# A two-layer hybrid decoder on one core: the 16 meta tokens' high and low parts as one stationary operand

## The chip, the core and the metric

The kernel runs on one core of a Trainium2 chip. The core has five engines that run side by side and meet only at semaphores: TensorE (PE, with its weight loads shown apart as PEld), VectorE (DVE), ScalarE (ACT), GpSimd (POOL) and SyncE (SP), which issues the loads of the weights. The metric is the device time of one execution in microseconds (us), and the time of a kernel is the median of several executions.

## What is computed

Two layers, each of them attention beside a convolution, then an MLP. The residual stream has 528 tokens: 16 learned meta tokens and the 512 of the sequence. The part that the change touches is the projection to queries, keys and values and what reads them:

```
u = rms_norm(h, norm_mix[l])
proj = u @ w_in[l]
glu_in, q, k, v, gates = jnp.split(proj, SPLITS, axis=-1)
...
q = apply_rope(rms_norm(q.reshape(B, Lp, N_HEADS, 2, HEAD_DIM), q_norm[l]), cos, sin)
k = apply_rope(rms_norm(k.reshape(B, Lp, N_HEADS, 2, HEAD_DIM), k_norm[l]), cos, sin)
...
o = diff_attention(q, k, v, lam)
...
h = h + merged @ w_o[l]
u = rms_norm(h, norm_mlp[l])
h = h + jnp.square(jax.nn.relu(u @ w_up[l])) @ w_down[l]
```

The width is 1024, there are 8 heads with two softmaxes each, and the output has the 512 sequence tokens of the last layer only.

## The kernel before

**Three products for one.** TensorE reads float32 operands here as float32r. To keep accuracy, every operand is held as a high part and a low part, and a product is made of three matmuls: high by high, low by high, high by low. `u[:, 0]` and `u[:, 1]` are the high and low parts of the normed input (transposed, channels on partitions), `w_hi` and `w_lo` those of a slab of weights, which is 1024 x 256 values. A slab comes by DMA into `w_raw`; for the query, key and value slabs ACT writes `w_hi` (`w_high_part`, a cast of 128 x 2048 values), and then POOL writes `w_lo` in 16 pieces (`split_low`) and announces the slab with `w_ready`. There are two buffers of each, so slab s+2 is split after slab s has been used, while slab s+1 is read.

**The tiles.** A pair of heads has three slabs, v, q and k. `b_tiles` lists tiles of tokens for each slab: tile 0 holds the 16 meta tokens, tiles 1 to 4 hold 128 tokens each. `b_tile` makes one: 8 blocks of the contraction by three matmuls, 24 in all, with a piece of `u` as the stationary operand (128 x 16 for tile 0, 128 x 128 for the others) and 256 columns of weights moving. The last layer has no meta queries, so meta tiles are 12 in layer 0 (v, q, k of four pairs) and 8 in layer 1 (v, k): 20 in all. Tiles go to two PSUM banks in turn. ACT evicts each (`b_evict`): a value tile with one scaled copy, a query or key tile with a copy to `raw` and four Squares with an accumulated sum, and then it releases the bank with `b_free`. After the last tile of a slab ACT casts the high part of slab s+2.

**The order.** Stage 0 of a layer is tiles alone, back to back. In stages 1 to 3 the tiles of pair p are strewn among the attention of pair p-1, and in stage 4 tiles of the gates (G) take their place. The order is written out in `MATRIX_ORDER`, and ACT follows the same list through `schedule`; DVE has a list of its own, `VECTOR_ORDER`, which the change leaves alone. In the list T is the next tile (T< and T> its halves), q and k0, k1 are transposes of rotated queries and keys, s, e, t, pv and y are the steps of a head: s01 is the scores of the pair's first head, group 1 (PE), e01 their exps (ACT), t00 and t01 the two halves of the transposes of the probabilities (PE, evicted by ACT to `a_t`), pv the product with the values, y the sums for the norm. Between s and e stands DVE's maximum (`maxima`, which ends with `nb`), and all scores use one pair of banks, so that scores of group n+1 wait until the exps of group n are done (`exp_done`). DVE's `combine` makes the probabilities after the third group. The keys take DVE and POOL after the last tile of the slab: norm statistics, `turn` on POOL, `rope` on DVE, and only then does POOL split the next slab.

The lines of the profile are those of the file before: L714 is the matmul of `b_tile`, L744 and L752 those of `scores`, L764 the transposes of the probabilities, L776 and L781 the product with the values, L702 sums over channels, L936 the eviction of a value tile, L945 and L949 of a query or key tile, L960 the cast of the high part, L995 the eviction to `a_t`, L973 and L978 the exps, L522 and L515 the low parts on POOL, L1235 the end of the keys' rotation on DVE.

## Time and profile before

| | |
|---|---|
| median of 3 runs | 1857.86 us (1855.82 to 1861.81) |
| the profiled execution | 1856.81 us, span 1855.0 us |
| granted TensorE clock | 0.999 of full speed |
| PE busy | 1831.2 us, 99% of the span, 12787 matmuls |
| PEld / POOL / DVE / ACT busy | 89% / 72% / 60% / 31% |
| query, key, value tiles (L714), PE busy | 337.1 + 259.7 us |

The profile is one execution. Busy time of matmuls overlaps, since a matmul is drained while the next one streams, so what a matmul costs is read from the distance between starts. In the chain of work that ended last PE holds 87% of the span and POOL 7%.

### The profile page before, as it was taken

How to read it: one execution, taken by the hardware profiler on the slowest of the kernel's cores; microseconds unless marked ns; L12 is line 12 of the kernel's file. 1: busy time of each engine (PE TensorE's matmuls, PEld its weight loads, DVE VectorE, ACT ScalarE, POOL GpSimd, SP SyncE). 2: the span in 40 equal slices, each digit the busy share in tenths (PEclk: the TensorE clock that was granted, in tenths of full speed). 3: DMA queues.
4: the chain of work that ended last, by engine and by line, in shares of the span. 5: the costliest groups of instructions: out<-in, count | busy, mean ns of one | idle time of the engine just before them, and what ended most of it. 6: DMA issues, size and time to landing. Idle time of an engine off the chain costs nothing.

```text
span 1855.0 us, 34632 instructions
## 1 busy us (share of the span) xinstructions
PE 1831.2 (99%) x12787; PEld 1652.2 (89%) x12787; DVE 1119.0 (60%) x1666; ACT 577.0 (31%) x1616; POOL 1333.3 (72%) x2400
## 2 busy tenths in 40 slices
PE   9999999999999999999999999999999999999999
PEld 9999888898999999999999998887768877888887
DVE  7998887877544333333468989888885433333233
ACT  4135565536332110101011246664362322010100
POOL 3767454646778888888898663436477799898985
PEclk9999999999999999999999999999999999999999
DMA  4221021112322222222232211111124222222222
GB/s 178 91 92 66 28 69 47 47 69 85 135 96 79 86 93 90 91 91 106 109 120 91 91 69 47 69 47 48 67 91 146 105 91 91 91 91 91 90 107 74
DMA packets 25550, 160.66 MB, mean 87 GB/s; under 512 B 3024, under 2 KB 3408, under 8 KB 7776
## 3 DMA queue, kind: packets, MB, share of 16 engines
q1 hardware_dynamic: 21888, 147.01, 22.4%
q10 hardware_dynamic: 3552, 12.15, 1.7%
q8 instruction: 73, 1.20, 0.3%
q14 instruction: 37, 0.30, 0.1%
HBM read 154.85 MB, written 4.29 MB: 86 GB/s over the span
## 4 chain that ended last, share of the span: by engine, by line
PE 87%; POOL 7%; DVE 2%; issue 2%; ACT 2%; POOLq 0%; DVEq 0%; ACTq 0%
PE psum L625 63%; PE psum L714 15%; POOL w_lo L515 4%; PE psum L744 2%; PE psum L776 2%; PE psum L764 1%; POOL w_lo L522 1%; POOL w_hi L513 1%; ACT e L978 1%; PE psum L752 1%; DVE mx L1259 1%; PE psum L646 1%; PE psum L821 1%; PE psum L793 1%; PE psum L632 0%
## 5 line engine op out<-in xcount | busy, mean ns | idle before, releaser
L625 PE MATMUL psum<-u,w_hi 128*128 128x264 f32 (+1 forms) x4416 | 900.5, 316 | 9.7 <-POOL w_lo L515 5.6
L515 POOL TENSOR_TENSOR w_lo<-w_raw,w_hi 128x128 fp32r<-128x128 f32 x1504 | 759.9, 543 | 7.8
L625 PEld LDWEIGHTS psum<-u,w_hi 128*128 128x128 f32 x4416 | 666.8, 189 | 68.1 <-issue 9.1
L625 PE MATMUL psum<-u,w_lo 128*128 128x264 f32 (+1 forms) x2208 | 558.8, 313 | 0.0
L522 POOL TENSOR_TENSOR w_lo<-w_raw,w_hi 128x128 fp32r<-128x128 f32 x640 | 314.3, 530 | 123.1 <-ACT w_hi L960 83.8
L625 PEld LDWEIGHTS psum<-u,w_lo 128*128 128x128 f32 x2208 | 362.5, 189 | 25.0
L714 PE MATMUL psum<-w_hi,u 128*128 128x256 f32 (+1 forms) x1856 | 337.1, 284 | 2.6 <-ACT v_sb L936 1.5
L467 DVE SCALAR_TENSOR_TENSOR psum<-xg,pvec,psum 128x512 f32<-128x512 f32 x440 | 300.9, 751 | 4.6 <-DVE xg L1399 2.2
L714 PEld LDWEIGHTS psum<-w_hi,u 128*128 128x128 f32 (+1 forms) x1856 | 264.8, 172 | 11.5 <-issue 3.1
L714 PE MATMUL psum<-w_lo,u 128*128 128x256 f32 (+1 forms) x928 | 259.7, 280 | 0.0
L1562 DVE TENSOR_TENSOR relu<-relu 128x528 f32<-128x528 f32 (+1 forms) x64 | 66.2, 1034 | 234.8 <-ACT u L1154 119.7
L1152 ACT ACTIVATE relu<-psum 128x528 f32<-128x528 f32 (+1 forms) x64 | 38.7, 605 | 459.9 <-PE psum L625 459.9
L513 POOL TENSOR_SCALAR w_hi<-w_raw 128x2048 fp32r<-128x2048 f32 x94 | 180.4, 1919 | 0.0
L512 POOL TENSOR_TENSOR tick<-ones 128x1 f32<-128x1 f32 x94 | 19.8, 211 | 218.8 <-PE psum L625 196.4
L625 PE MATMUL psum<-hid_b,w_hi 128*128 128x264 f32 (+1 forms) x768 | 163.9, 322 | 0.1
L714 PEld LDWEIGHTS psum<-w_lo,u 128*128 128x128 f32 (+1 forms) x928 | 159.7, 172 | 3.7
L1591 DVE TENSOR_TENSOR down_tmp<-psum,r_inv 128x512 f32<-128x512 f32 (+1 forms) x56 | 39.1, 699 | 190.3 <-PE psum L625 190.3
L567 POOL TENSOR_TENSOR rtmp<-raw,tabs 128x640 f32<-128x640 f32 x16 | 25.0, 1562 | 153.1 <-DVE q_scale L1221 101.9
L625 PEld LDWEIGHTS psum<-hid_b,w_hi 128*128 128x128 f32 x768 | 118.7, 188 | 12.0 <-issue 0.6
L625 PE MATMUL psum<-hid_b,w_lo 128*128 128x264 f32 (+1 forms) x384 | 102.4, 321 | 0.0
L978 ACT ACTIVATE e<-psum,nb,q_scale 128x272 f32<-128x272 f32 (+4 forms) x144 | 83.8, 585 | 35.8 <-DVE nb L1265 35.8
L960 ACT CAST w_hi<-w_raw 128x2048 fp32r<-128x2048 f32 x40 | 76.6, 1915 | 48.6 <-PE psum L625 48.6
(190 smaller groups left out, 1963.0 us busy)
## 6 DMA issues: line engine op xcount, KB each, us to landing
w_raw<-w_slabs SPq DMA_DIRECT2D x135, 1024.0 KB, 4.9
h<-x_t SPq DMA_DIRECT2D x4, 528.0 KB, 7.2
h<-x_t ACTq DMA_DIRECT2D x1, 2112.0 KB, 10.7
h_spill<-h ACTq DMA_DIRECT2D x8, 264.0 KB, 2.2
h<-h_spill ACTq DMA_DIRECT2D x1, 2112.0 KB, 10.4
out<-h SPq DMA_DIRECT2D x8, 256.0 KB, 2.0
r_b<-r_rows ACTq DMA_DIRECT2D x1, 1584.0 KB, 6.5
r_b<-r_rows ACTq DMA_DIRECT2D x1, 1536.0 KB, 7.4
```

Source lines behind the costliest of these rows:

```text
L467: return nc.vector.scalar_tensor_tensor(out=done if ends else acc, in0=x, scalar=w, in1=done if begins else acc, op0=ALU.mult, op1=ALU.add)
L513: chain.link(nc.gpsimd.tensor_scalar(w_hi[:, b, :], w_raw[:, b, :], 1.0, 1.0, ALU.mult, ALU.mult))
L515: last = nc.gpsimd.tensor_tensor(w_lo[:, b, c:c + P], w_raw[:, b, c:c + P], w_hi[:, b, c:c + P], ALU.subtract)
L522: last = nc.gpsimd.tensor_tensor(w_lo[:, b, c:c + P], w_raw[:, b, c:c + P], w_hi[:, b, c:c + P], ALU.subtract)
L625: last = nc.tensor.matmul(psum[:, 2 * slot + j, 0:n], w[:, b, cut], src[:, part, kc, at0:at0 + n], start=(kc == 0 and m == 0), stop=(kc == ...
L714: last = nc.tensor.matmul(psum[0:tn, n % 2, 0:2 * P], u[:, part, kc, t0:t0 + tn], w[:, b, kc * 2 * P:(kc + 1) * 2 * P], start=(kc == 0 and ...
L744: nc.tensor.matmul(psum[0:tn, banks[c], at0:at0 + k1 - k0], qk[rows64, 0, hh % 2, qp, t0:t0 + tn], qk[rows64, 1, hh % 2, kp, k0:k1], start ...
L960: nc.scalar.copy(w_hi[:, b, :], w_raw[:, b, :]).then_inc(w_high, 1)
L978: ins = nc.scalar.activation(e[0:tn, c, E_OFF[i]:E_OFF[i] + w], psum[0:tn, banks[c], S_AT[i]:S_AT[i] + w], ACT.Exp, bias=nb[0:tn, c, i:i + ...
L1152: nc.scalar.activation(row(relu[:, j, :], layer), a_ps(layer, j), ACT.Relu).then_inc(a_free[j], 1)
L1562: link(V.tensor_tensor(relu2[:, lo:lo + n], relu[:, j, lo:lo + n], relu[:, j, lo:lo + n], ALU.mult))
L1591: announce(dve, V.tensor_tensor(row(down_tmp[:], layer), a_ps(layer, j), row(r_inv2[:], layer), ALU.mult), a_free[j], a_read(layer, A_MLP ...
```

## The change

The meta tokens are taken out of `b_tiles`, which now has tiles 1 to 4 of each slab. For v, q and k of layer 0 and v and k of layer 1 a meta product is opened ahead of tile 1 (`b_open`): the stationary operand is `meta_u`, 128 x 32, the high parts of the 16 tokens beside their low parts, and it meets `w_hi` and `w_lo`, 16 matmuls in place of 24. That gives 32 rows, 16 from the high parts and 16 from the low ones. ACT copies them to `meta_low` (`meta_evict`). A float32 matmul with two 16 x 16 identities stacked as the stationary operand (L744 of the new file) then adds the two halves into columns 256 to 511 of the bank of tile 2, right behind tile 2's first matmul, and tile 2's eviction takes the 16 rows along. `meta_low` and the stacked identities are float32, so that matmul is a plain float32 one.

Three things come with it. Each product with meta tokens holds one of the two banks from its opening until ACT has copied it; tile 1 goes to the other bank and tile 2 to that one. The cast for slab s+2 moves: where the following slab has meta tokens, ACT makes it behind `meta_evict` of that slab and not behind the last tile of its own. And `MATRIX_ORDER` is written anew for the stages "first" and "mid".

```diff
 def b_tiles(layer):
-    return [("v", t) for t in range(NTOK)] + [("q", t) for t in q_tiles(layer)] + [("k", t) for t in range(NTOK)]
+    return [(what, t) for what in "vqk" for t in range(1, NTOK)]
...
-MATRIX_ORDER = [{"first": "T q T T T k0 T< s00 k1 e00 T> T s01 T< e01 T> T s02 T< e02 T> T T< t00 s10 t01 e10 T> T s11 e11 pv0 T< s12 e12 T> y0 T T< t10 T> t11",
-     "mid": "T T pv- T q T k0 T s00 e00 T T s01 T< e01 y- T> k1 s02 e02 T T s10 t00 T< t01 e10 T> T s11 T< e11 T> T< s12 e12 pv0 T> T< y0 t10 T> t11",
+MATRIX_ORDER = [{"first": "T< q T> T T k0 T< s00 k1 e00 T> T< s01 T> e01 T s02 T< e02 T> T T< t00 s10 t01 e10 T> s11 e11 pv0 T< s12 e12 T> y0 T T< t10 T> t11",
+     "mid": "T pv- T q T k0 T s00 e00 T s01 T< e01 y- T> k1 s02 e02 T T s10 t00 T< t01 e10 T> s11 T< e11 T> T< s12 e12 pv0 T> T< y0 t10 T> t11",
...
-     "mid": "T T< pv- T> q T k0 T s00 k1 T< e00 T> y- s01 T< e01 T> T< s02 e02 T> T s10 t00 T< t01 e10 T> pv0 s11 T< e11 T> T s12 y0 e12 T T T< t10 T> t11",
+     "mid": "T pv- T< q T> k0 T s00 k1 T< e00 T> y- s01 T< e01 T> T< s02 e02 T> T s10 t00 t01 T< e10 T> pv0 s11 T< e11 T> s12 y0 e12 T T T< t10 T> t11",
...
+            def b_parts(n, b, t, first, last, opened):
+                t0, tn = TOK[t]
+                for k in range(first, last):
+                    part, w = [(0, w_hi), (1, w_hi), (0, w_lo)][k % 3]
+                    kc = k // 3
+                    done = nc.tensor.matmul(psum[0:tn, B_BANK[n], 0:2 * P], u[:, part, kc, t0:t0 + tn], w[:, b, kc * 2 * P:(kc + 1) * 2 * P],
+                                            start=k == 0, stop=k == 3 * NT - 1)
+                    if k == 0 and opened:
+                        nc.tensor.matmul(psum[0:META, B_BANK[n], 2 * P:4 * P], meta_low[0:2 * META, 2 * P:2 * P + META], meta_low[0:2 * META, 0:2 * P], start=False, stop=False)
+                return done
+            def b_open(layer, n, b):
...
+                for kc in range(NT):
+                    for w in (w_hi, w_lo):
+                        last = nc.tensor.matmul(psum[0:2 * META, bank, 0:2 * P], meta_u[:, kc, :], w[:, b, kc * 2 * P:(kc + 1) * 2 * P],
+                                                start=kc == 0 and w is w_hi, stop=kc == NT - 1 and w is w_lo)
+                last.then_inc(meta_full, 1)
...
+            def meta_evict(layer, pair, j, what):
...
+                act.wait_ge(meta_full, m + 1)
+                nc.scalar.copy(meta_low[0:2 * META, 0:2 * P], psum[0:2 * META, B_BANK[n + 1], 0:2 * P]).then_inc(meta_out, 1)
+                while high_due:
+                    w_high_part(layer, high_due.pop())
...
                 if t == NTOK - 1:
-                    w_high_part(layer, s + 2)
+                    following = "qkv"["vqk".index(what)]
+                    if with_meta(layer, following) and (what != "k" or pair < 3):
+                        high_due.append(s + 2)
+                    else:
+                        w_high_part(layer, s + 2)
...
+                act.wait_ge(u_ready, (layer * 2 + 1) * NT)
+                nc.scalar.copy(meta_u[:].rearrange("p k (a m) -> p k a m", a=2), u[:, :, :, 0:META].rearrange("p a k m -> p k a m")).then_inc(meta_in, 1)
...
+                announce(dve, V.tensor_tensor(meta_low[0:2 * META, 2 * P:2 * P + META], ident[0:2 * META, 0:META], ident[0:2 * META, META:2 * META], ALU.add), meta_sum, layer + 1)
```

On ACT, the place of the keys of pair 1 in layer 0 (stage 2), from the end of the fourth query tile to the first exp of the pair's second head. `a_t` is the transposed probabilities, `squares` a scratch of the norm sums. Before:

```order
L949 ACTIVATE squares,ssq<-psum 128x64 x3
L960 CAST w_hi<-w_raw 128x2048 [waits w_landed1]
L995 COPY a_t<-psum 128x512 [waits t_full] x2
L995 COPY a_t<-psum 128x256 [waits t_full]
L997 COPY a_t<-psum 16x16
L995 COPY a_t<-psum 16x512 [waits t_full]
L978 ACTIVATE e,es<-psum,nb,q_scale 128x272 [waits t_full,max_ready]
```

And now:

```order
L1031 ACTIVATE squares,ssq<-psum 128x64 x3
L1081 COPY a_t<-psum 128x512 [waits t_full] x2
L989 COPY meta_low<-psum 32x256 [waits meta_full]
L1046 CAST w_hi<-w_raw 128x2048 [waits w_landed1]
L1081 COPY a_t<-psum 128x256 [waits t_full]
L1083 COPY a_t<-psum 16x16
L1081 COPY a_t<-psum 16x512 [waits t_full]
L1064 ACTIVATE e,es<-psum,nb,q_scale 128x272 [waits t_full,max_ready]
```

The cast has moved from ahead of the first `a_t` copies to between the two halves of them, behind a copy that waits for the opened keys.

On ACT again, the keys of pair 1 in layer 1 (stage 2), from the product with the values (evicted to `o_t`) to the exps of the second head's group 1, which begin with those of `s_tail`. Before:

```order
L949 ACTIVATE squares,ssq<-psum 128x64 x3
L960 CAST w_hi<-w_raw 128x2048 [waits w_landed1]
L1014 ACTIVATE o_t<-psum,sub_g 128x512 [waits t_full]
L1015 ACTIVATE o_sq<-psum 128x512
L973 ACTIVATE e,es<-s_tail,nb,q_scale 128x16 [waits max_ready]
```

And now:

```order
L1031 ACTIVATE squares,ssq<-psum 128x64 x3
L1100 ACTIVATE o_t<-psum,sub_g 128x512 [waits t_full]
L1101 ACTIVATE o_sq<-psum 128x512
L989 COPY meta_low<-psum 32x256 [waits meta_full]
L1046 CAST w_hi<-w_raw 128x2048 [waits w_landed1]
L1059 ACTIVATE e,es<-s_tail,nb,q_scale 128x16 [waits max_ready]
```

The cast stands directly ahead of these exps now, and it waits for PE to have opened the keys, which PE does after the scores of group 1.

On PE, the start of tile 2 of the values in stage 0 of layer 0, with the new matmul behind the first of the tile:

```order
L741 MATMUL psum<-w_hi,u 128x256 [waits meta_out,meta_sum,w_ready]
L744 MATMUL psum<-meta_low 16x256
L741 MATMUL psum<-w_hi,u 128x256
L741 MATMUL psum<-w_lo,u 128x256
L741 MATMUL psum<-w_hi,u 128x256 x2
```

In the tile before the change the first two rows of `w_hi` followed each other without it.

## Rows read from the trace of the kernel before

**Rows 1.** The page, part 1: busy time, share of the span and instructions.

```profile
PE 1831.2 (99%) x12787; PEld 1652.2 (89%) x12787; DVE 1119.0 (60%) x1666; ACT 577.0 (31%) x1616; POOL 1333.3 (72%) x2400
```

**Rows 2.** Groups by shape: line, stationary and moving sizes, count | busy us, mean ns | idle before.

```profile
L714 PE MATMUL psum<-w_hi,u 128*16 128x256 f32 x320 | 58.1, 282 | 0.8 <-POOL w_lo L522 0.8
```

**Rows 3.** Timeline of PE, stage 0 of layer 0: start, us, line, shapes, count.

```profile
122.87 0.40 PE L714 MATMUL psum<-w_hi,u 128*16 128x256 f32 x2
...
125.66 0.40 PE L714 MATMUL psum<-w_hi,u 128*128 128x256 f32 x2
...
128.49 0.40 PE L714 MATMUL psum<-w_hi,u 128*128 128x256 f32 x2
```

**Rows 4.** Timelines of PE and PEld where plain float32 matmuls stand.

```profile
432.80 7.37 PE L702 MATMUL psum<-ln_sq,ones 128*128 128x264 f32 x32
439.81 0.85 PE L625 MATMUL psum<-u,w_hi 128*128 128x264 f32 x4
...
1186.67 3.37 PE L776 MATMUL psum<-a_t,v_sb 128*128 128x512 f32 x10
1189.97 0.97 PE L744 MATMUL psum<-qk 64*128 64x512 f32 x6
...
197.70 0.19 PEld L776 LDWEIGHTS psum<-a_t,v_sb 128*128 128x128 f32 x1 [0.24 <-issue]
```

**Rows 5.** Waits of PE over the whole span: in total, times, longest.

```profile
PE psum L744 <- ACT e L978: 3.1, 9, 0.5
...
PE psum L714 <- ACT v_sb L936: 1.5, 2, 0.7
...
PE psum L714 <- POOL w_lo L522: 1.1, 2, 0.8
```

**Rows 6.** Timelines of POOL and PE, stage 1 of layer 0: the second query slab.

```profile
162.83 7.60 POOL L522 TENSOR_TENSOR w_lo<-w_raw,w_hi 128x128 fp32r<-128x128 f32 x16 [4.75 <-DVE raw L1235]
...
170.49 0.41 PE L714 MATMUL psum<-w_hi,u 128*16 128x256 f32 x2 [0.82 <-POOL w_lo L522]
```

**Rows 7.** Timelines of ACT and PE, stage 1 of layer 0: last exp of group 0, scores.

```profile
195.45 0.18 ACT L978 ACTIVATION_READ_ACCUMULATOR e<-psum,nb,q_scale 16x1 f32 x1
...
196.19 0.97 PE L744 MATMUL psum<-qk 64*128 64x512 f32 x6
```

**Rows 8.** Timeline of ACT, stage 2 of layer 0, around the first keys.

```profile
255.07 1.93 ACT L960 CAST w_hi<-w_raw 128x2048 fp32r<-128x2048 f32 x1
256.87 1.11 ACT L995 COPY a_t<-psum 128x512 f32<-128x512 f32 x2
258.60 0.37 ACT L995 COPY a_t<-psum 128x256 f32<-128x256 f32 x1 [0.63 <-PE psum L764]
...
259.54 0.57 ACT L978 ACTIVATE e<-psum,nb,q_scale 128x272 f32<-128x272 f32 x1
...
262.15 0.19 ACT L978 ACTIVATION_READ_ACCUMULATOR e<-psum,nb,q_scale 16x1 f32 x1
```

**Rows 9.** Timeline of PE in the same stretch.

```profile
256.52 0.48 PE L714 MATMUL psum<-w_hi,u 128*16 128x256 f32 x2
...
258.00 1.02 PE L764 MATMUL psum<-ident,e 128*128 128x128 f32 x7
258.78 0.48 PE L714 MATMUL psum<-w_hi,u 128*16 128x256 f32 x2
...
263.18 0.97 PE L744 MATMUL psum<-qk 64*128 64x512 f32 x6
```

**Rows 10.** Timelines of PE and ACT, stage 2 of layer 1, around the first keys.

```profile
1190.96 0.42 PE L714 MATMUL psum<-w_hi,u 128*16 128x256 f32 x2
...
1196.71 0.81 PE L744 MATMUL psum<-qk 64*128 64x400 f32 x6
...
1193.17 0.40 ACT L973 ACTIVATE e<-s_tail,nb,q_scale 128x16 f32<-128x16 f32 x1 [1.24 <-DVE nb L1265]
...
1195.37 0.19 ACT L978 ACTIVATION_READ_ACCUMULATOR e<-psum,nb,q_scale 128x1 f32 x1
```

**Rows 11.** Timeline of PE, stage 1 of layer 1: second transposes right behind the first.

```profile
1125.38 1.00 PE L764 MATMUL psum<-ident,e 128*128 128x128 f32 x6 [0.38 <-ACT a_t L995]
```

More of the change, by code:

```diff
@@ L422, in b_read_wait @@
             for k in range(2):
-                eng.wait_ge(b_free[k], (n + 1 - k) // 2)
+                eng.wait_ge(b_free[k], B_USES[n][k])
         def round_wait(eng, n):
@@ L704, in channel_sums @@
                 last.then_inc(done, 1)
-            def b_tile(layer, n, b, t, half):
+            def b_parts(n, b, t, first, last, opened):
                 t0, tn = TOK[t]
-                if n >= 2 and half != 1:
-                    pe.wait_ge(b_free[n % 2], n // 2)
-                for kc in range(NT) if half is None else range(half * NT // 2, (half + 1) * NT // 2):
-                    for m, (part, w) in enumerate([(0, w_hi), (1, w_hi), (0, w_lo)]):
-                        last = nc.tensor.matmul(psum[0:tn, n % 2, 0:2 * P], u[:, part, kc, t0:t0 + tn], w[:, b, kc * 2 * P:(kc + 1) * 2 * P],
-                                                start=(kc == 0 and m == 0), stop=(kc == NT - 1 and m == 2))
+                for k in range(first, last):
[6 more added lines that the diff above has]
+                return done
@@ new lines, in b_tile @@
+            def b_tile(layer, n, b, t, half, meta):
+                bank = B_BANK[n]
+                opened = int(meta is not None and t == 2)
+                if meta is not None and t == 1:
+                    if half != 1:
+                        b_open(layer, n + 1, b)
+                    cuts = 0, 0, 3 * NT
+                else:
+                    cuts = 0, 3 * NT // 2, 3 * NT
+                lo, hi = cuts[1 if half == 1 else 0], cuts[1 if half == 0 else 2]
+                if lo == hi:
+                    return
+                if opened and half != 1:
+                    pe.wait_ge(meta_sum, layer + 1)
+                    pe.wait_ge(meta_out, meta + 1)
+                elif lo == 0 and B_USES[n][bank]:
+                    pe.wait_ge(b_free[bank], B_USES[n][bank])
+                last = b_parts(n, b, t, lo, hi, opened)
@@ L866, in _ @@
                             pe.wait_ge(w_ready, slab + 1)
-                            b_tile(layer, n + x, slab % 2, t, c[0])
+                            b_tile(layer, n + x, slab % 2, t, c[0], metas_before(layer, stage, what) if with_meta(layer, what) else None)
                         elif step == "gate":
@@ L929, in b_evict @@
                     act.wait_ge(b_full, n + 1 - (layer * N_QKV + 3 * pair + "vqk".index(what)))
+                meta = with_meta(layer, what) and t == 2
+                bank = B_BANK[n]
                 if what == "v":
-                    if t == 0 and (layer or pair > 1):
+                    if t == 1 and (layer or pair > 1):
                         before = ("pv", layer, 2 * pair - 3) if pair > 1 else ("pv", layer - 1, HEADS - 1)
```

58 lines of the change are left out of this document (48 added, 10 removed), and 2 rows, old and new, of the table MATRIX_ORDER.

## The prediction

> **What bounds the kernel now.** I read part 1 of the page first: PE is busy for 99% of the span [rows 1], so a microsecond of PE work is worth up to a microsecond, and any pause of PE costs its length. Next the waits of PE: those in the attention stages are few and short, at most 0.8 us each [rows 5]. They name what stands close behind PE there: the exps on ACT, the value evictions on ACT, the low parts on POOL. PE is thus the bound, but with little cover left on the others. The question for this change is which of the exp chains, that run scores, maximum, exps, next scores, lose the tiles that hide them. I answer it place by place from the timelines of PE and ACT. All sums are against the profiled execution of 1856.81 us, which lies 1.05 us below the median; the same difference is then put on the median.
>
> **What the matmuls give back.** A meta tile is 24 matmuls with a 16-column stationary operand, 320 + 160 of them in all for 20 tiles [rows 2]. It takes 125.66 - 122.87 = 2.79 us, a tile of 128 tokens 128.49 - 125.66 = 2.83 us [rows 3]. So a matmul of 256 columns costs 0.1165 to 0.118 us whatever the width of the stationary operand, and 32 columns will cost the same. Opening takes 16 of them: 8 fewer are 0.94 us per meta tile, 18.8 us for 20. The Trainium skill (TensorE: Matmul & The Clock Gate, Back-to-back issue gap) gives the columns over 2.4 GHz plus 2.5 ns, 0.109 us for 256; by that alone the 20 tiles would give 17.5 us, but the trace's distance of 0.1175 us decides.
>
> **What the identity matmul takes.** The trace has no lone float32 matmul of 256 columns between float32r ones. Plain float32 matmuls are recorded as two each. The 32 of L702 take 439.81 - 432.80 = 7.01 us, 0.219 us each for 264 columns, so 0.438 us for one matmul and 0.427 us for 256 columns. Five of L776, with 1792 columns, take 1189.97 - 1186.67 = 3.30 us, where 1792 columns at that rate are 2.97: 0.07 us more each [rows 4]. Coming back to float32r costs about 0.07 us: the half tile at 256.52 takes 1.48 us for 12 matmuls [rows 9], where 12 x 0.1175 are 1.41. I take 0.55 us. From below the bound is 0.43, the streaming alone. From above it is 0.99: 0.43 plus two pauses of 0.24 us, as weight loads of L776 show them [rows 4], plus 0.08. The Trainium skill (FP8 and Floating Point Precision, TensorE Precision Notes) has true float32 as four passes through the array, 0.427 us for 256 columns; with nothing for the change of type the sum would be about 1.8 us lower than mine.
>
> Net, a meta tile that is wholly on the path gives 0.94 - 0.55 = 0.39 us.
>
> **Stage 0.** Tiles back to back. No wait for a bank is recorded there, and the only one between tiles that is, behind value evictions, comes from stages 2 and 3 [rows 5]; I take it that tile 2's eviction, longer by the meta rows, still fits into the 2.8 us tile behind it. Three meta tiles in layer 0 and two in layer 1 give 5 x 0.39 = -1.95 us.
>
> **Stage 1, values and queries.** The value tile gives nothing. The second query slab is split only after the keys' rotation, which hangs on the end of the previous key tile: POOL starts at 162.83, behind L1235, and PE waits 0.82 us for it at 170.49 [rows 6]. A shorter value slab makes that wait longer by as much. In layer 1 the same wait is 0.3 us (the second of the two in [rows 5]) and takes the same gain. The query tile of layer 0 gives -0.39.
>
> **Stage 1, keys, layer 0.** Between the second head's scores of group 0 and group 1 there were 36 matmuls of tiles and there will be 24: -1.41 us of cover. The exps end at 195.45 + 0.18 = 195.63, PE started group 1 at 196.19 [rows 7], 0.56 us later. For the way of a semaphore I allow 0.14 us (POOL's end at 170.43 and PE's start at 170.49 show 0.06 [rows 6]). PE will come about 1.4 us earlier and wait 0.95 to 1.0 us. Keys: -0.94 + 0.55 + 0.97 = +0.58.
>
> **Stages 2 and 3, layer 0.** The values gain more than tiles. Before, both banks were full of value tiles that ACT may not evict until the product with the values is done, and PE waited 0.7 us for that, twice [rows 5]. The opened meta product is copied without waiting, so its bank is free: -0.39 - 0.73 = -1.12. Queries: -0.94, and the identity matmul falls where PE waited 0.34 us for exps anyway (the mean of nine such waits [rows 5]), so it costs 0.21: -0.73. Keys are the place that decides. Before, ACT made the cast at 255.07, ahead of the `a_t` copies, where it had time, copied the second half of `a_t` at 258.60 when PE delivered it, and began the exps at 259.54 [rows 8]. Now the cast stands behind the copy of the opened keys. PE opens at 256.52, and 16 matmuls with the switch take 1.95, so until 258.47; the last starts at 258.35, lasts 0.28 [rows 2] and ends at 258.63, the copy starts at 258.67, the cast 0.26 later at 258.93 (a copy of 0.37 us [rows 8], of which 0.1 overlaps the next instruction, as the cast's last 0.13 does), and the next instruction 1.80 us after it (256.87 - 255.07) at 260.73. The copies take 0.94 (259.54 - 258.60), the exps 2.80 (to 262.34) [rows 8]: they end at 264.47, and PE may go on at 264.61. PE itself arrives at 263.18 - 0.94 = 262.24 [rows 9]. A new wait of 2.37 us. In the group after, the identity matmul takes the place of a wait of 0.38. Keys: -0.94 + 2.37 + 0.17 = +1.60. A stage: -1.12 - 0.73 + 1.60 = -0.25, two stages -0.5.
>
> **Layer 1, keys of stage 1.** No 12 matmuls are lost ahead of group 1; the identity falls on a wait of 0.46 us (the longest in [rows 5]), and a wait of about 0.3 for the probabilities comes up since 12 matmuls fewer lie between group 2 and their transposes. I put -0.4.
>
> **Stages 2 and 3, layer 1.** Values: -0.39. The halves of the transposes now follow each other. Where they did so before, PE waited 0.38 us for ACT [rows 11], and the four transposes of the last round, which wait for a second copy, took some 0.4 more: +0.8. Keys: the scores of group 1 start at 1189.97 [rows 4], the opening at 1190.96 [rows 10] and lasts 1.90; copy at 1193.06, cast at 1193.32, and the exps of group 1 can start at 1195.12. Before, they started at 1193.17 and ended at 1195.56, 2.39 later [rows 10]. So they end at 1197.51, PE may go on at 1197.65, and it arrives at 1196.71 - 0.94 = 1195.77: a new wait of 1.88. Keys: -0.94 + 0.55 + 1.88 = +1.49. A stage: -0.39 + 0.8 + 1.49 = +1.9, two stages +3.8.
>
> **The rest.** 20 copies to `meta_low` (0.26 us each, as above) and 20 evictions of meta rows lie on ACT, 31% busy [rows 1]; beyond the places above they are covered. Without cover one costs 0.3 us. The copy to `meta_u` and the sum of identities stand on ACT and DVE between the GLU steps; together 0 to 0.4 us, I take 0.1. The casts come 0.4 to 6 us later, and POOL still ends these slabs 3 us or more before PE wants them. Query slabs hang on the rotation, not the cast. Stage 4 and the MLP follow PE and move with it.
>
> **Sum.** -1.95 (stage 0) - 0.39 + 0.58 (stage 1, layer 0) - 0.5 - 0.4 + 3.8 + 0.1 = +1.2 us. So 1858.0 us for the profiled execution and 1859.1 for the median. The matmuls give back 18.8 us, the identity matmuls take 11, and new waits take the rest.
>
> **Rivals.**
> *The cast does no harm.* If the exps behind it are not late (ACT is nearer to PE's end of the opening than I read, or there is cover that I miss), four waits go, 2 x 2.37 + 2 x 1.88 = 8.5 us: 1850.6. For it: the lists were written anew at just these places. Against it: the order of instructions on ACT is fixed, and the cast needs 1.8 us [rows 8] between two things that PE waits for.
> *The identity matmul is dear.* At 0.99 us each, 0.44 more on the 14 that are wholly exposed and the 4 that only fill a wait: 18 x 0.44 = 7.9 us, 1867.0, slower. For it: the weight loads of L776 do pause 0.24 us [rows 4], and a float32 matmul among float32r ones changes type twice. Against it: the five of L776 pay 0.07 us each. It decides from about 0.8 us each, where the sum passes 0.3%.
> *The saving isn't there.* If a matmul with 32 columns and alternating `w_hi` and `w_lo` cost more than 0.1175 us, say 0.13, 320 of them add 4 us: 1863. Rows 3 speak against it.
>
> **How the numbers follow.** About 0.3% (5.6 us) is what a measurement of this kernel can tell from no change. Forecast, with the sizes of its waits a little off, 0.55: 1855.5 to 1863. Harmless casts 0.17. Dear identities 0.12. Dearer opening 0.06. The remaining 0.10 is a wait I have not found, or a place where less is lost, spread over both sides. For a range with no more than 2 in 10 outside, I go down to the second case and leave out the third and most of the tail above: 1850.0 to 1865.0. Faster by over 0.3% (below 1852.3): 0.18. Slower by over 0.3% (above 1863.4): 0.18. Within: 0.64.
>
> **What would show it.** In the profile after, PE's busy time falls by some 8 us while the span stays. PE waits for the exps in total of some 6 to 9 us, against 3.1, with waits of 2.4 us in stages 2 and 3 of layer 0 at group 1 of the second head and of 1.9 us in layer 1 at its group 2. The waits for the value eviction are gone. The wait for the second query slab in layer 0 grows to about 1.2 us. The distance from tile 2's first matmul to its third is 0.55 us longer. I am wrong if the casts don't stand ahead of late exps, or if the identity matmul costs above 0.8 us.

## The result: slower by 0.7%

The kernel after the change takes 1871.19 us (median, 1870.47 to 1873.31), the kernel before 1856.93 us over all its runs beside it; the ratio is 1.0072 (95% interval 1.006 to 1.0084). The forecast was 1859.1 us with a range of 1850.0 to 1865.0, and the measured time lies 6.2 us above that range. A repeat (e9 below) gave 1869.92 against 1857.34, ratio 1.0069.

Part 1 of the page of the kernel after, against [rows 1]:

```profile
PE 1837.3 (98%) x12667; PEld 1651.6 (88%) x12667; DVE 1120.1 (60%) x1668; ACT 584.3 (31%) x1638; POOL 1333.0 (71%) x2400
```

PE has 120 instructions fewer and is busy 6 us longer. So waits alone don't explain the time: the same work has become dearer somewhere. The waits of PE after, against [rows 5] (L806 is the scores, L826 the transposes of the probabilities, L755 the opening):

```profile
PE psum L806 <- ACT e L1064: 9.4, 8, 2.1
...
PE psum L826 <- ACT a_t L1081: 1.9, 5, 0.4
...
PE psum L755 <- POOL w_lo L551: 0.8, 1, 0.8
```

The waits for exps have grown from 3.1 to 9.4 us in total, and the one for value evictions is gone, both as forecast in kind. The chain behind the long waits is the one of the prediction too. Timeline of ACT after, stage 2 of layer 0, against [rows 8]: start, us, line, operation.

```profile
255.94 0.36 ACT L989 COPY meta_low<-psum 32x256 f32<-32x256 f32 x1 [1.11 <-PE psum L755]
256.20 1.90 ACT L1046 CAST w_hi<-w_raw 128x2048 fp32r<-128x2048 f32 x1
258.01 0.36 ACT L1081 COPY a_t<-psum 128x256 f32<-128x256 f32 x1
...
258.81 0.57 ACT L1064 ACTIVATE e<-psum,nb,q_scale 128x272 f32<-128x272 f32 x1
...
261.43 0.19 ACT L1064 ACTIVATION_READ_ACCUMULATOR e<-psum,nb,q_scale 16x1 f32 x1
```

PE in the same place, against [rows 9]:

```profile
259.33 0.28 PE L741 MATMUL psum<-w_lo,u 128*128 128x256 f32 x1
261.76 1.62 PE L806 MATMUL psum<-qk 64*128 64x512 f32 x6 [2.14 <-ACT e L1064]
...
263.94 1.03 PE L744 MATMUL psum<-meta_low 32*16 32x256 f32 x2
264.90 0.58 PE L741 MATMUL psum<-w_hi,u 128*128 128x256 f32 x1
...
270.90 0.82 PE L806 MATMUL psum<-qk 64*128 64x400 f32 x6
```

The exps end at 261.62, and the scores begin 0.14 us later, after a wait of 2.14 us. What the prediction doesn't have is on the same rows. The six score matmuls take 1.62 us where they took 0.97 [rows 9], the identity matmul is recorded with 1.03 us (0.60 in stage 0), and the 35 tile matmuls from 264.90 to 270.90 take 6.00 us where 35 x 0.1175 are 4.11. PE ran at half clock behind the pause. Stretches of 12 us from each of the four long waits, after, with the first of them before as the last line: busy us of PE, PEld, DVE, ACT, POOL, then the granted clock.

```profile
261.00:273.00 12.00, 11.24 (x57) 8.53 (x58) 6.82 (x10) 6.27 (x39) 5.73 (x14) 0.72 0.26 89
332.00:344.00 12.00, 11.55 (x58) 9.04 (x59) 6.45 (x11) 5.98 (x38) 4.50 (x11) 0.72 0.25 87
1202.00:1214.00 12.00, 11.31 (x67) 10.01 (x68) 9.85 (x17) 5.25 (x33) 5.01 (x13) 0.72 0.25 87
1269.00:1281.00 12.00, 11.83 (x85) 11.04 (x86) 10.38 (x18) 5.94 (x41) 4.50 (x11) 0.86 0.25 87
```

```profile
261.00:273.00 12.00, 11.62 (x82) 9.43 (x81) 10.88 (x16) 8.40 (x45) 6.72 (x12) 1.00 0.26 87
```

A clock of 0.72 over 12 us is work for 3.4 us not done, 0.86 is 1.7 us. In slices of 4 us the clock reads 0.50 behind three of the waits, which is 1.2 GHz. That makes 3 x 3.4 + 1.7 = 11.9 us. The kernel before loses 1.7 us in this way, once, behind a wait of 2.37 us for DVE that ends at 31.37 us. But it also waits 1.83 us for POOL in the MLP of layer 1, as long as the two new waits of layer 1, and keeps the whole clock there. Both rows, and 12 us around each:

```profile
31.37 1.03 PE L625 MATMUL psum<-u,w_hi 128*128 128x264 f32 x3 [2.37 <-DVE glu_a L1390]
...
1390.24 0.73 PE L625 MATMUL psum<-u,w_hi 128*128 128x512 f32 x2 [1.83 <-POOL w_lo L515]
```

```profile
28.00:40.00 12.00, 9.63 (x68) 9.42 (x67) 6.48 (x9) 2.76 (x3) 5.98 (x11) 0.86 0.25 89
1387.00:1399.00 12.00, 10.17 (x45) 7.92 (x44) 6.38 (x9) 6.37 (x8) 9.88 (x20) 1.00 0.23 87
```

Lengths of the stretches between the same points of both kernels (us):

| stretch | before | after | difference | of it half clock | forecast |
|---|---|---|---|---|---|
| start to the first tiles | 108.75 | 107.42 | -1.33 | -1.7 | +0.1 |
| layer 0, stage 0 | 42.31 | 41.82 | -0.49 | 0 | -1.17 |
| layer 0, stage 1 | 62.17 | 62.87 | +0.70 | 0 | +0.19 |
| layer 0, stage 2 | 67.50 | 70.48 | +2.98 | +3.4 | -0.25 |
| layer 0, stage 3 | 68.23 | 71.85 | +3.62 | +3.4 | -0.25 |
| to the tiles of layer 1 | 699.99 | 700.06 | +0.07 | 0 | 0 |
| layer 1, stage 0 | 39.52 | 39.08 | -0.44 | 0 | -0.78 |
| layer 1, stage 1 | 58.80 | 58.23 | -0.57 | 0 | -0.4 |
| layer 1, stage 2 | 61.22 | 66.47 | +5.25 | +3.4 | +1.9 |
| layer 1, stage 3 | 62.58 | 65.89 | +3.31 | +1.7 | +1.9 |
| the rest | 583.93 | 584.13 | +0.20 | 0 | 0 |
| sum | 1855.0 | 1868.3 | +13.3 | +10.2 | +1.2 |

Without the clock the difference is 3.1 us, where the forecast had 1.2.

### The profile page after: what moved, and what is told of

Same layout as the page of the kernel before. It is cut to its first block, busy times and chain, and to the rows that moved or that the text cites. A ratio compares the mean times of both kernels' runs of the same rounds, so it can differ in the third digit from the quotient of the medians.

```text
span 1868.3 us, 34398 instructions
## 1 busy us (share of the span) xinstructions
PE 1837.3 (98%) x12667; PEld 1651.6 (88%) x12667; DVE 1120.1 (60%) x1668; ACT 584.3 (31%) x1638; POOL 1333.0 (71%) x2400
## 3 DMA queue, kind: packets, MB, share of 16 engines
q8 instruction: 72, 1.18, 0.3%
## 4 chain that ended last, share of the span: by engine, by line
PE 86%; POOL 6%; issue 2%; ACT 2%; DVE 2%; DMA 0%; POOLq 0%; DVEq 0%; ACTq 0%
PE psum L654 62%; PE psum L741 13%; POOL w_lo L544 4%; PE psum L838 2%; PE psum L806 2%; PE psum L755 2%; POOL w_lo L551 1%; PE psum L826 1%; ACT e L1064 1%; POOL w_hi L542 1%; PE psum L814 1%; PE psum L855 1%; PE psum L675 1%; PE psum L883 1%; PE psum L744 1%
## 5 line engine op out<-in xcount | busy, mean ns | idle before, releaser
L741 PE MATMUL psum<-w_hi,u 128*128 128x256 f32 x1536 | 294.1, 291 | 0.7 <-POOL w_lo L551 0.7
L741 PEld LDWEIGHTS psum<-w_hi,u 128*128 128x128 f32 x1536 | 242.9, 193 | 12.5 <-issue 11.2
L741 PE MATMUL psum<-w_lo,u 128*128 128x256 f32 x768 | 218.5, 284 | 0.0
L741 PEld LDWEIGHTS psum<-w_lo,u 128*128 128x128 f32 x768 | 148.5, 193 | 0.0
```

The costliest lines, as they stand in the source:

```text
L741: done = nc.tensor.matmul(psum[0:tn, B_BANK[n], 0:2 * P], u[:, part, kc, t0:t0 + tn], w[:, b, kc * 2 * P:(kc + 1) * 2 * P], start=k == 0, ...
```

## The experiments

My theory: the moved cast makes four pauses of PE (7.9 us), the pauses bring half clock behind them (10 to 12 us), and together with a dearer identity matmul this eats what the matmuls give back. Rivals: the clock falls because of something else in the changed kernel (the plain float32 matmul, the mix of types, the new order), or the pauses are only where the time happens to show.

**e1: the cast back.**

```diff
                 if t == NTOK - 1:
-                    following = "qkv"["vqk".index(what)]
-                    if with_meta(layer, following) and (what != "k" or pair < 3):
-                        high_due.append(s + 2)
-                    else:
-                        w_high_part(layer, s + 2)
+                    w_high_part(layer, s + 2)
```

> The kernel after the change, with ACT's cast of the high part put back to where it stood before: behind the last tile of its own slab, not behind the copy of the opened meta product. All else is as changed. My theory is that the 14 us come from the moved cast: four waits of PE for late exps (2.14, 2.14, 1.81 and 1.81 us in the profile after), and the half clock that the profile shows behind each of them (6.8 us of half clock three times and 3.4 us once, which costs up to 3.4 x 3 + 1.7 = 12 us). It expects those four waits to be under 0.5 us, the granted clock back at 0.998 or more, and 1851 to 1856 us. A rival, that the new order of the tiles and the plain float32 identity matmuls make the time and the cast only fell beside them, expects waits of the same sum somewhere else, or the half clock to stay, and 1864 us or more.

Measured: 1856.27 us (1854.08 to 1857.55), against 1857.12 for the kernel before beside it, ratio 0.9997 (0.9988 to 1.0007). The page's waits for exps, and 16 us around the first of the four places:

```profile
PE psum L806 <- ACT e L1060: 3.5, 8, 0.9
```

```profile
260.00:276.00 16.00, 15.40 (x107) 12.30 (x106) 13.51 (x24) 11.22 (x60) 6.60 (x12) 1.00 0.19 68
```

In layer 0 the waits shrink to 0.60 us, not quite under the 0.5 I had written; in layer 1 they are 0.15 us. The time lies 0.3 us above the 1851 to 1856 that I expected. The clock is whole at all four places. One edit on ACT takes back 14.9 us, all of the loss of 14.3. The moved cast is the cause; by which way it is not shown yet.

**e2 and e11: the pauses filled.** The casts stay where they do harm; PE only gets something to do while it waits. `fill` is 18 and 15 (layer 0, layer 1) in e2 and 9 and 7 in e11, in stages 2 and 3 for the keys.

```diff
+                for k in range(fill if meta is not None and t == 1 and half == 1 else 0):
+                    nc.tensor.matmul(psum[0:tn, bank, 0:2 * P], u[:, k % 2, k % NT, t0:t0 + tn], w_hi[:, b, k % NT * 2 * P:(k % NT + 1) * 2 * P], start=k == 0, stop=k == fill - 1)
                 last = b_parts(n, b, t, lo, hi, opened)
```

> The kernel after the change, with idle matmuls put in front of the four waits: ahead of the first key tile in stages 2 and 3, PE makes 18 (layer 0) or 15 (layer 1) redundant matmuls of the same shape and type as the tile's, 2.1 and 1.8 us of them, as long as the waits were; their result is overwritten. The casts stay where the change put them, the exps are as late as before. If the half clock is a consequence of PE standing still there, it goes: the waits fall to near 0, the granted clock is 0.998 or more, and although PE has 66 matmuls more to do the time is 9 to 12 us lower than the kernel after, 1859 to 1863 us. If the clock has another cause (the identity matmul, the mix of types), nothing is gained: 1870 to 1872 us with a clock of 0.994.

Measured: 1863.38 us (1859.66 to 1864.62), 7.8 us less than the kernel after, with 66 matmuls more. The same 16 us:

```profile
260.00:276.00 16.00, 15.99 (x112) 13.04 (x111) 11.94 (x23) 12.16 (x60) 7.49 (x16) 1.00 0.20 68
```

The clock is 1.00 at all four places. The gain is below the 9 to 12 us expected, since in the profiled execution PE lost 1.7 us each at two other places (near 32 us, as in the kernel before, and near 1396 us, behind a wait of 1.87 us for POOL that all kernels here have). The execution with the highest clock, 1.000, took 1859.66. Work in place of waiting keeps the clock, with the identity matmuls, the types and the order all left as changed. That excludes the first rival.

> The kernel after the change with half of the redundant matmuls ahead of the late scores: 9 in stages 2 and 3 of layer 0, 7 in those of layer 1, so that PE's four waits shrink to about 1.1, 1.1, 1.0 and 1.0 us while the scores start as late as ever. The whole fill left no wait there and no half clock and gave 1863.4 us. If it is enough to halve the pauses, the clock is whole again, 0.998 or 0.999, and the time is that of the whole fill, 1862 to 1864 us. If pauses of 1 us lose the clock as those of 2 us do (one of 1.07 us did so in the old kernel, and one of 1.70 us did not), it stays at 0.993 to 0.996 and 1867 to 1872 us.

Measured: 1864.55 us (1863.03 to 1867.45) at a clock of 0.996 to 0.998. Its waits are 1.07, 1.06, 0.97 and 0.99 us. Windows of 12 us from the first and from the last:

```profile
262.00:274.00 12.00, 11.79 (x76) 9.06 (x77) 9.41 (x19) 8.27 (x44) 4.28 (x11) 1.00 0.26 89
...
1260.00:1272.00 12.00, 11.49 (x69) 10.19 (x70) 10.03 (x18) 5.11 (x34) 4.83 (x12) 0.72 0.27 87
```

Three of the four pauses of 1 us cost nothing beyond themselves, and one cost 3.4 us. The median lies between the two expectations, 0.6 us above the range of the first: half the pause was usually short enough, not always.

**e4 and e7: pauses in the old kernel.** The kernel before, meta tiles and all, with small chained copies on ACT ahead of the second head's exps; `pad` is a scratch of its own. The counts shown are those of e4; e7 has 12, 12, 18 and 18.

```diff
             def exps(layer, hh, n):
...
+                for _ in range({(0, 3, 0): 10, (0, 5, 0): 6, (1, 3, 1): 14, (1, 5, 1): 10}.get((layer, hh, n), 0)):
+                    link(nc.scalar.copy(pad[:], ones[:, 0:32]))
                 act.wait_ge(max_ready, step + 1)
```

> The kernel before the change, whose meta tiles are untouched, with small chained copies on ACT ahead of the exps of the second head: group 0 of it in layer 0 (10 copies in stage 2, 6 in stage 3), group 1 in layer 1 (14 and 10). I estimate 0.3 us for each, so PE should wait for exps about 2.1 and 1.0 us in layer 0 and 2.0 and 0.8 us in layer 1, where before it waited less than 0.5. My theory, that a pause of PE is followed by half clock whatever the kernel does otherwise, expects half clock behind the long two at least, 1.7 to 3.4 us lost for each beyond the pause: 6 us of pauses and 4 to 10 us of clock, 1866 to 1872 us. The shorter two tell what a pause of 1 us does. The rival, that only the changed kernel's matmuls lose the clock, expects the pauses alone, 1861 to 1864 us, at a clock of 0.999.

Measured: 1862.22 us (1861.63 to 1863.71), clock 0.997 or 0.998. Two of its waits and the 12 us around each:

```profile
265.24 0.97 PE L745 MATMUL psum<-qk 64*128 64x512 f32 x6 [1.70 <-ACT e L981]
...
1200.54 0.81 PE L745 MATMUL psum<-qk 64*128 64x400 f32 x6 [1.07 <-ACT e L981]
```

```profile
264.00:276.00 12.00, 10.76 (x71) 8.54 (x72) 9.07 (x20) 8.94 (x47) 3.97 (x10) 1.00 0.26 88
...
1198.00:1210.00 12.00, 10.93 (x81) 10.50 (x80) 9.30 (x18) 7.37 (x40) 3.65 (x9) 0.86 0.26 87
```

My expectation failed: the time lies in the range that I had written for the rival (1861 to 1864), the longest pause kept the clock and a shorter one lost it. One loss of 1.7 us in the old kernel doesn't decide between the two. The copies were shorter than estimated, too (0.25 us each), so the pauses came out at 1.70, 0.70, 1.07 and none.

> The kernel before the change again with chained small copies on ACT ahead of the exps of the second head, now 12 in both stages of layer 0 and 18 in both of layer 1. The run with 10, 6, 14 and 10 copies gave waits of 1.70, 0.70, 1.07 and none, and half clock behind one of them alone, the 1.07 us in layer 1. Per copy that is 0.24 to 0.25 us, so these should give four waits of about 2.2, 2.2, 2.0 and 2.0 us, 8.4 us and a little more than the 7.9 us of the changed kernel. If such pauses lose the clock in the old kernel as in the new one, another 7 to 12 us come with them, the granted clock is 0.993 to 0.995 and the time 1872 to 1878 us. If the clock falls only sometimes, as the first run of this kind has it, 1867 to 1872. If the changed kernel's clock fell for another reason, 1865.5 us at 0.999.

Measured: 1869.88 us (1867.88 to 1871.07), ratio 1.0064 (1.0049 to 1.0079), clock 0.995 to 0.997. The waits are 2.21, 2.21, 2.08 and 2.08 us.

```profile
264.00:276.00 12.00, 11.53 (x65) 9.34 (x66) 8.07 (x16) 7.62 (x42) 2.68 (x7) 0.86 0.25 87
335.00:347.00 12.00, 11.60 (x79) 9.40 (x80) 9.63 (x21) 8.76 (x46) 2.57 (x7) 1.00 0.24 89
1203.00:1215.00 12.00, 11.29 (x70) 11.06 (x71) 9.37 (x17) 5.80 (x37) 0.81 (x2) 0.72 0.24 87
1270.00:1282.00 12.00, 11.80 (x89) 11.57 (x90) 10.36 (x19) 6.69 (x43) 0.29 (x1) 0.86 0.22 88
```

The old kernel, made to wait in the same places, is nearly as slow as the new one. Half clock came behind three of four pauses and cost 1.7 + 3.4 + 1.7 = 6.8 us. That is under the 7 to 12 that I expected for "as in the new kernel", and the time fits the middle case, 1867 to 1872: the clock falls often, not always. The rival's 1865.5 us at a clock of 0.999 is out.

**e3, e6 and e10: what the identity matmul costs.** Timeline of the kernel after, stage 0, tile 2 of the values:

```profile
112.07 0.28 PE L741 MATMUL psum<-w_hi,u 128*128 128x256 f32 x1
...
112.28 0.60 PE L744 MATMUL psum<-meta_low 32*16 32x256 f32 x2
112.81 0.19 PEld L741 LDWEIGHTS psum<-w_hi,u 128*128 128x128 f32 x1 [0.42 <-issue]
112.81 0.39 PE L741 MATMUL psum<-w_hi,u 128*128 128x256 f32 x1
...
113.05 0.28 PE L741 MATMUL psum<-w_lo,u 128*128 128x256 f32 x1
```

Three distances are long: 0.21 ahead of the matmul, 0.53 its own, 0.24 behind. Without the identity matmul the way from 112.07 to 113.05, 0.98 us, would be 2 x 0.1175. The price is 0.75 us, where the prediction had 0.55.

```diff
-        meta_low = at("meta_low", [P, 2 * P + META], F32, base)
+        meta_low = at("meta_low", [P, 2 * P + META], F32R, base)
```

> The kernel after the change, with meta_low and the stacked identities as float32r, so that the matmul that adds the halves goes through once and without a change of type. That rounds the meta tokens' queries, keys and values; nothing else is changed. It prices the identity matmul in place. The prediction put 0.55 us on it, the profile after shows about 0.76 in stage 0. As float32r it should cost about the 0.12 us of the others, 0.64 less by the profile's figure and 0.43 less by the prediction's. 20 of them, of which 14 to 18 stand on the path: 9 to 11.5 us less than the kernel after by the first, 6 to 8 by the second, and the stretch of stage 0 between tile 1's start and tile 3's shorter by 0.64 or 0.43 us. The waits behind the cast and the half clock stay, since the cast stays. If the identity were nearly free already, the time would stay at 1871.

Measured: 1864.86 us (1863.66 to 1865.55), 6.3 us less than the kernel after. The meta tokens' queries, keys and values are rounded here, and in e5, e8 and e12 below, which they are in neither of the two kernels; those times belong to a less exact computation.

```profile
112.43 0.28 PE L741 MATMUL psum<-w_hi,u 128*128 128x256 f32 x1
112.64 0.29 PE L744 MATMUL psum<-meta_low 32*16 32x256 f32 x1
112.86 0.39 PE L741 MATMUL psum<-w_hi,u 128*128 128x256 f32 x1
113.08 0.28 PE L741 MATMUL psum<-w_lo,u 128*128 128x256 f32 x1
```

From 112.43 to 113.08 are 0.65 us, so the price is 0.42, not the 0.12 of its neighbours. By its total the run would have confirmed a price of 0.55 with nothing left afterwards; the rows say 0.75 with 0.42 left. I went by the rows and asked what the 0.3 us are.

```diff
-                        nc.tensor.matmul(psum[0:META, B_BANK[n], 2 * P:4 * P], meta_low[0:2 * META, 2 * P:2 * P + META], meta_low[0:2 * META, 0:2 * P], start=False, stop=False)
+                        nc.tensor.matmul(psum[0:META, B_BANK[n], 2 * P:4 * P], meta_low[:, 2 * P:2 * P + META], meta_low[:, 0:2 * P], start=False, stop=False)
...
+                for p in (32, 64, 96):
+                    link(V.tensor_scalar(meta_low[p:p + 32, 0:2 * P], ident[p:p + 32, 0:1].to_broadcast([32, 2 * P]), 0.0, None, ALU.mult))
```

The sum of the identities is made over all 128 rows as well.

> The kernel after the change, with the identity matmul over 128 rows in place of 32: the stacked identities have zeros below row 32, and the rows of meta_low below 32 are zeroed by DVE once in a layer. It stays plain float32, and the result is the same. In the profile after, three distances around this matmul are longer than the others: 0.21 us ahead of it, 0.53 its own, 0.24 behind it, against 0.1175 each for the matmuls around; together it costs 0.75 us. As float32r the three are 0.21, 0.22 and 0.22, so 0.3 us of the price are left although type and passes are those of its neighbours. My reading is that these 0.3 us come from its 32 rows standing between matmuls of 128 rows, since the weight load of the next matmul starts only with that matmul. Then the distances next to it fall to about 0.12 and the price to 0.43 to 0.5 us: 20 x 0.25 to 0.3, of which 16 stand on the path, 4 to 5 us less than the kernel after, 1866 to 1867 us. If the price belongs to a lone matmul with another stationary operand, the distances stay and so does the time, 1870.5 to 1872 us.

Measured: 1866.35 us (1865.0 to 1870.33). The total is as expected, but the rows refute the reason:

```profile
114.09 0.28 PE L741 MATMUL psum<-w_hi,u 128*128 128x256 f32 x1
114.30 0.60 PE L744 MATMUL psum<-meta_low 128*16 128x256 f32 x2
114.84 0.38 PE L741 MATMUL psum<-w_hi,u 128*128 128x256 f32 x1
115.06 0.28 PE L741 MATMUL psum<-w_lo,u 128*128 128x256 f32 x1
```

The distances are 0.21, 0.54 and 0.22, as with 32 rows, and stage 0 takes 41.80 us against 41.82. The four executions had clocks of 0.993, 0.997, 0.996 and 0.995 and took 1870.33, 1865.0, 1865.56 and 1867.15 us. So I ran it again beside the kernel after.

> The kernel after the change as it is, on the chip and in the hours of the other three of this call. Its first runs had 1870.5 to 1873.3 us at a granted clock of 0.992 to 0.994; the runs with the same waits but another identity matmul had 0.993 to 0.997. If the half clock behind the waits comes every time, this gives 1870 to 1873 again. If it comes by chance from run to run, the clock is spread from 0.993 to 0.997 here too, and the time with it, 1865 to 1873 us, about 1.3 to 1.9 us for each thousandth of the clock.

> The kernel after the change with the plain float32 identity matmul over 128 rows, once more and beside the kernel after itself. The first time its median was 4.8 us below the kernel after, but its profile shows the three long distances around the identity unchanged (0.21, 0.54 and 0.22 us) and every stage as long as before the edit, and its four runs spread from 1865.0 to 1870.3 us as the clock went from 0.997 to 0.993. My reading now is that the row count does nothing while the matmul is plain float32, and that the 4.8 us are the clock's. Then it is within 2 us of the kernel after where both have the same clock. If the rows were worth something outside what the rows of stage 0 show, it is 4 to 5 us lower at the same clock.

Measured: 1869.92 us (1869.31 to 1870.52, clocks 0.993 to 0.995) for the kernel after and 1867.93 us (1866.34 to 1869.52, 0.994 to 0.996) for the one with 128 rows. The distance between the two has shrunk from 4.8 to 2.0 us, about what the clock differs by. In the kernel after the clock was not spread as far as 0.997: all its executions, eight now, lie between 0.992 and 0.995, which is the case "every time" of the expectation, with a median 0.1 us below the 1870 written there. The profiled spans less what half clock took (next table) are 1855.9 and 1857.1 us: no gain from the rows. Whether the last 2 us of the medians are chance stays open.

**e5, e8 and e12: together.**

> Two edits together on the kernel after the change: the cast back where it stood, and meta_low and the stacked identities as float32r, which rounds the meta tokens' queries, keys and values. Alone the first gave 14.9 us (1856.3) and the second 6.3 us (1864.9). If they are independent costs, as my theory has it, the sum is 1871.2 - 14.9 - 6.3 = 1850.0 us, 1848.5 to 1851.5, and the granted clock is 0.999. If the float32r edit gained mostly because the half clock was shorter in it (its profile shows less of it behind the two waits of layer 0), then little of the 6.3 is left once the clock is whole: 1853 to 1855 us.

Measured: 1851.20 us (1849.26 to 1852.0), ratio 0.9965 (0.9951 to 0.9979). With the cast back the float32r edit keeps 5.1 of its 6.3 us (1856.27 - 1851.20).

> All three edits on the kernel after: cast back, identity matmul as float32r (which rounds the meta tokens' queries, keys and values), and over 128 rows. If the row count is what the lone matmul pays for, it costs no more than its neighbours here, 0.12 us, and the three distances around it are all 0.12: 0.3 us x 16 to 20 less than with the first two edits, so 4.8 to 6 us below their 1850: 1844 to 1846 us, 0.6 to 0.7% faster than the kernel before. If the row count does nothing, it is the time of the two edits, 1850.

Measured: 1846.23 us (1845.28 to 1848.05), ratio 0.9941 (0.9927 to 0.9954).

```profile
113.98 0.28 PE L741 MATMUL psum<-w_hi,u 128*128 128x256 f32 x1
114.10 0.28 PE L744 MATMUL psum<-meta_low 128*16 128x256 f32 x1
114.22 0.28 PE L741 MATMUL psum<-w_hi,u 128*128 128x256 f32 x1
114.33 0.28 PE L741 MATMUL psum<-w_lo,u 128*128 128x256 f32 x1
```

Now all three distances are 0.11 or 0.12. Each edit alone leaves gaps of 0.21 and 0.22 around the matmul; both together remove them. The loads of the stationary operands show the same: in e8 that of the identity and that of the matmul behind it start at 113.99 and 114.10, one matmul ahead of their own, while in the kernel after both start only with their matmuls (112.28 and 112.81). The row count does cost something, but it shows only when the type is right.

```diff
-     "mid": "T pv- T< q T> k0 T s00 k1 T< e00 T> y- s01 T< e01 T> T< s02 e02 T> T s10 t00 t01 T< e10 T> pv0 s11 T< e11 T> s12 y0 e12 T T T< t10 T> t11",
+     "mid": "T pv- T< q T> k0 T s00 k1 T< e00 T> y- s01 T< e01 T> T< s02 e02 T> T s10 t00 T< t01 e10 T> pv0 s11 T< e11 T> s12 y0 e12 T T T< t10 T> t11",
```

> The fastest version so far (cast back, identity matmul as float32r over 128 rows, which rounds the meta tokens' queries, keys and values, 1846.2 us), with half a query tile put between the two halves of the transposes of the probabilities in stages 2 and 3 of layer 1, as in the kernel before. In the prediction the adjacent halves cost 0.8 us a stage; the profiles show 0.39 us of wait for ACT's copy there. If the prediction's term is right, 1.6 us less, 1844.6; if only the recorded wait counts, 0.8 less, 1845.4; if the time comes back as a wait for the exps that now start later, 1846 or more.

Measured: 1843.59 us (1843.31 to 1844.43), ratio 0.9928 (0.9914 to 0.9942), faster than both kernels. The meta tokens are rounded, as said at e3. Stage 2 of layer 1 takes 60.22 us against 61.06 in e8: 0.84 less, the prediction's term of 0.8, of which 0.39 is a recorded wait. Stage 3 gains only 0.37 us (60.49 against 60.86 from its start to the recorded wait that follows it): a wait of 0.41 us for the probabilities stands where that of 0.39 for ACT's copy stood. The span fell by 2.3 us. Of these, 0.9 lie in stage 1 of layer 0, where nothing was edited: the profiled execution of e8 waits 0.94 us for exps at 170.53, and that of e12 0.09. So the order is worth 1.2 us here, not the 1.6 of the prediction.

The profiled executions side by side (the median of the kernel before is the one beside e1 to e4). "Lost" is (1 - clock) x 4 us, summed over all slices of 4 us with a clock below 0.99, without the end of the span, where the clock falls in all of them.

| kernel | median us | span | lost | span less lost |
|---|---|---|---|---|
| before | 1857.1 | 1855.0 | 1.7 | 1853.3 |
| after | 1871.2 | 1868.3 | 11.9 | 1856.4 |
| e1 cast back | 1856.3 | 1854.0 | 1.7 | 1852.3 |
| e2 whole fill | 1863.4 | 1861.2 | 3.4 | 1857.8 |
| e11 half fill | 1864.6 | 1860.9 | 3.4 | 1857.5 |
| e3 float32r identity | 1864.9 | 1863.4 | 11.9 | 1851.5 |
| e4 old, short pauses | 1862.2 | 1860.6 | 3.4 | 1857.2 |
| e7 old, long pauses | 1869.9 | 1868.3 | 6.8 | 1861.5 |
| e5 cast back, float32r | 1851.2 | 1847.5 | 1.7 | 1845.8 |
| e6 128 rows | 1866.4 | 1868.5 | 11.9 | 1856.6 |
| e9 after, again | 1869.9 | 1867.8 | 11.9 | 1855.9 |
| e10 128 rows, again | 1867.9 | 1867.4 | 10.2 | 1857.1 |
| e8 three edits | 1846.2 | 1844.4 | 1.7 | 1842.7 |
| e12 and order | 1843.6 | 1842.1 | 1.7 | 1840.4 |

In e2, e3, e5, e6 and e9, 1.7 of the lost us stand near 1390 us, behind the wait of 1.8 us for POOL, and not in the attention stages. The last column is a check on the reading: e2 and e11, which only trade waiting for work, stand within 1.4 us of the kernel after, and e7 exceeds the kernel before by 8.2 us, where its waits for exps grew by 7.9 us, from 3.1 [rows 5] to 11.0.

## Why the prediction was wrong

**What bounds the kernel**: right. PE is the bound and the exp chains are its rivals.

**What the matmuls give back**: right. The opening's 16 matmuls stand 0.11 to 0.12 us apart, and tile 1 starts 1.83 us behind the opening (107.42 to 109.25 in stage 0) where 16 x 0.1175 are 1.88.

**The identity matmul**: the size was off, 0.75 us measured against 0.55, well inside the bounds 0.43 to 0.99. Streaming is 0.43 of it, and 0.32 us come on top where the prediction had 0.12. Its sentence "Coming back to float32r costs about 0.07 us" and the "0.07 us more each" of L776 are too low for a lone matmul. The second is a mean over five that follow one another: singly, the first four share 0.13 us, and the last, ahead of the scores, has 0.20 (it starts at 1188.92, the scores at 1189.97, and 512 columns stream in 0.85). On the 18 that I counted as exposed 0.2 us each are 3.6 us, an estimate. Stage 0 shows the loss undisturbed: -0.49 and -0.44 where the forecast had -1.17 and -0.78. The rival of the dear identity put its price at 0.99 and its turning point at 0.8; neither was reached.

**Stage 1**: +0.70 and -0.57 against +0.19 and -0.4. The predicted wait for exps ahead of the second head's group 1 came, 0.66 us instead of 0.97, and that for the second query slab is 0.84 us where I had some 1.2. In layer 1 no new wait for the probabilities came. Where the 0.5 us above the forecast lie in layer 0 is not located.

**The moved cast**: right in place and mechanism, and nearly in size. Waits of 2.14, 2.14, 1.81 and 1.81 us against 2.37 and 1.88. The value evictions' waits are gone, as said. The adjacent halves of the transposes cost 0.84 us in stage 2 of layer 1 and 0.37 in stage 3 by e12, forecast 0.8 each. The sign "in total of some 6 to 9 us" of waits for exps was put lower than the sum's own new waits, 2 x 2.37 + 2 x 1.88 + 0.97 = 9.5 us; the page has 9.4.

**The step that failed** is what the sum does with these waits: "a new wait of 2.37 us" was entered at 2.37. It cost PE that time and then 1.7 or 3.4 us more, since the clock stood at half behind it. The trace of the kernel before shows that this can happen: PE waits 2.37 us near 31 us and loses 1.7 us at half clock, while behind the 1.83 us near 1390 us the clock stays whole. The prediction reads the waits of the attention stages and neither of those. With 10.2 us of clock the profiled execution comes out of my sum at 1858.0 + 10.2 = 1868.2, and the actual 1870.47 lies 2.3 us above. Of the rest stage 0 shows 1.0 us, the identity matmuls alone; how the remainder splits between them and small terms of either sign is not shown. That the cast and not something else is behind waits and clock together is shown by e1. That the pauses bring the clock's fall is shown by e2, which fills them with work and leaves all else as changed, and by e7, which makes them in the old kernel. Why pauses of equal length bring it in one place nearly always and in another seldom stays open.

**"PE's busy time falls by some 8 us"**, the first sign that I named: it rose by 6 instead. That number alone would have told that PE runs slower and not only waits longer.

**The rival "the cast does no harm"** gave 1850.6 us for four waits gone. With the cast back they are gone or 0.60 us, and e1 has 1856.3. So its total was too low as well, by 5.7 us; waits of 0.60 us twice and the identities' 3.6 us (the estimate above) are most of that.

## What to carry to other kernels

On a kernel whose TensorE is 99% busy, a new wait of about 2 us has to be entered with its length and with the chance of half clock behind it; here that more than doubled the price (7.9 us of waits, 11.9 us of clock). Look in the trace of before for every wait of that length and read the granted clock behind each, in several executions if there are any: one that fell is a warning, and one that didn't is no all-clear. A step that an engine off the path makes "at a quieter time" belongs behind what TensorE waits for, and a lone matmul between others is cheapest with their type and their number of rows (0.12 us in place of 0.75 here), if the rounding can be borne.

## What the hardware showed

**Pauses and the clock.** One profiled execution each of before, after and e1 to e12, with the waits of PE by place (the first 10 us left out):

| place | length, us | half clock behind it |
|---|---|---|
| attention stages, changed kernel and variants | 1.80 to 2.14 | 20 of 20 |
| attention stages, old kernel (e7) | 2.08 to 2.21 | 3 of 4 |
| attention stages, old kernel (e4) | 1.70 | 0 of 1 |
| attention stages, for exps (e4, e11) | 0.97 to 1.07 | 2 of 5 |
| attention stages of layer 1, for POOL (e2, e5) | 1.13 and 1.17 | 0 of 2 |
| near 31 us, for DVE | 2.27 to 2.61 | 8 of 14 |
| MLP of layer 1, near 1390 us, for POOL | 1.82 to 1.87 | 5 of 14 |
| 13 us ahead of that one, for POOL | 1.42 to 1.56 | 0 of 14 |
| MLP of layer 0, near 475 us, for POOL | 1.05 to 1.18 | 0 of 14 |

Behind waits of 0.95 us and less it never fell. Each fall cost 1.7 or 3.4 us of work. Ahead of the waits in the first four lines PE had worked for 6.6 us or more without a wait, at 2.4 GHz; ahead of those near 1390 us it had worked for 11.4 us. So neither the length of the wait nor a long unbroken stretch before it settles whether the clock falls.

**A lone matmul between others.** 256 columns among float32r matmuls of 128 rows, added time: plain float32 with 32 rows 0.75 us, plain float32 with 128 rows 0.74, float32r with 32 rows 0.42, float32r with 128 rows 0.12. Type and rows are not additive: either one that differs costs the gaps on both sides. The Trainium skill (TensorE: Matmul & The Clock Gate, Why this matters for your kernels) says that a single matmul with K=32 takes the same time as one with K=128. For its own stretch the rows agree in plain float32 (0.53 and 0.54), but among float32r neighbours of 128 rows the 32 rows cost 0.30 us more here.
